# Latent attention on TensorE: the product of weights and values, from full precision to three products of high and low parts

## The chip, the cores and the metric

The kernel runs on one core of one Trainium2 chip. The metric is the device time of one execution in microseconds (us). A core has a matrix engine (TensorE, PE in the profile, with its weight loads shown apart as PEld), a vector engine (VectorE, DVE), an activation engine (ScalarE, ACT), GpSimd (POOL) and the queue that issues DMAs (SyncE, SP). The engines run their own instruction streams side by side and wait for one another by semaphores.

## The reference, cut to what matters

The reference is two transformer blocks over 512 latent and 256 context tokens, then a routed layer of experts. The change is in the second layer of the first block, a latent attention of 8 heads over all 768 tokens as keys:

```python
def mla_core(q, k, v):
    s = jnp.einsum('bqhd,bkhd->bhqk', q, k).astype(F32) * ((C_NOPE + C_ROPE) ** -0.5)
    p = jax.nn.softmax(s, axis=-1)
    return jnp.einsum('bhqk,bkhd->bqhd', p.astype(v.dtype), v)

def keys_values(ckv, k_rope, length):
    kv = (rms_norm(ckv, kv_norm_w) @ wkv_b).reshape(bsz, length, C_HEADS, C_NOPE + C_V)
    ...
```

Queries and keys have 128 + 64 features to a head, values 128. The second `einsum` of `mla_core` (weights times values) is what the change computes in another way.

## The kernel before, in words

Everything is float32 in memory. A product of two float32 matrices is made in one of two ways. In the first, the operands are declared F32 and TensorE does the multiplication in full precision; the trace then has two MATMUL records (and two LDWEIGHTS records) for each such instruction of the program. In the second, each operand is split into a high part (ScalarE copies the value into a tile of the type F32R, which rounds it) and a low part (VectorE subtracts the high part from the value), and TensorE makes three F32R products: high by high, high by low, low by high. Each of these has one record. The large projections (`three`, lines 2106 to 2108) and the scores of this attention (`odd_scores`, lines 2309 and 2316) are made in the second way. The product of weights and values (line 2292) is made in the first.

The latent attention handles the 8 heads in two groups `g` of four. For each group PE makes queries (`q`, six column blocks), their rotations (`rope`), keys (`kv`, four blocks) and values (`v`, six token tiles of 512 columns). ScalarE makes high parts of queries and keys, VectorE their low parts (`low`, line 1592); the values are only copied by ScalarE into `v_o` (line 1047).

Then come 16 units, one for each of four query tiles and four heads, handled in pairs by `attend_pairs`. For a pair PE runs: six transposes of the exponentials `po` for each unit (jobs "T", line 2160), the scores of the next pair (jobs "S", `odd_scores`), and six products of transposed weights with values for each unit (jobs "O", line 2292). Around it, VectorE takes the maximum of each row of scores (`maximum`, line 1530), ScalarE takes the exponential (`exps`, line 1022) into `po`, and copies each finished transpose from PSUM into `pto` (line 1055); VectorE scales the output by the reciprocal of the sum (`scaled_out`, lines 1536 and 1538). PSUM has four slots of two banks. `begin` of a job waits until the job before it in its slot was evacuated. The units' "S" jobs use slots 0 and 1; "T" and then "O" of a unit share slot 2 or 3, so an "O" waits for the evacuation of its own unit's "T".

VectorE and ScalarE are strictly in order. VectorE's list for a pair is: two maxima of the next pair, two `scaled_out`, in group 1 for every second pair a multiplication of a row tile by the gate (line 1625), and then side work: for the first two pairs of a group the low parts of the weights streamed for later stages (`low_part`, line 1246), for the next six partial sums for a modulation vector (`add_part`, lines 1291 and 1293). The last pair of a group has no scores of a next pair between its "T" and its "O".

The stages after this attention (projection out, second block, experts) start only from its output rows `oo_rows`.

Of the kernel before, what the change touches and what calls it, by code (L numbers as in the profile page):

```python
# [16 lines left out]
P = 128  # L17
# [275 lines left out]
def build(nc, src, out):  # L293
# [8 lines left out]
    with ExitStack() as stack:  # L302
# [58 lines left out]
        v_o = at("v_o", g_base, 0, [P, NT, 512])  # L361
# [7 lines left out]
        po, pto = [], []  # L369
        for g in range(2):  # L370
            used = plan.splits[plan.through["q", g] - 1]["k"] % SPLIT
            po.append(at(f"po{g}", split_base, 8 * KB * used, [P, 3, TOK]))
            pto.append(at(f"pto{g}", split_base, 8 * KB * (SPLIT + used), [P, 2, TOK]))
        y_in = at("y_in", split_base, 8 * KB * (SPLIT + used) + 8 * KB, [P, 2, D])

        qa = at("qa", g_base, 0, [P, LT, 512])
        kk = at("kk", g_base, 8 * KB, [P, NT, 512])
# [477 lines left out]
        def _(act):  # L855
# [160 lines left out]
            def exps(stage, u, pbuf, nb):  # L1016

                if u % S_RUN[stage] >= 3:
                    filled(act, "T", stage, u - 3)
                act.wait_ge(nb, u + 1)  # L1020
                st = soft[:, u % 4, :]
                own.free(nc.scalar.activation(pbuf[:, u % 3, :], slot(("S", stage, u))[:, 0:TOK], ACT.Exp, bias=st[:, 1:2],
                                         accum_out=st[:, 2:3]), ev("S", stage, u))

            for g in range(2):
                for f in Q_ORDER:
                    v = filled(act, "q", g, f)
                    if f < 4:
                        own.free(nc.scalar.activation(q_h[:, f, :], v[:, 0:SEQ], ACT.Copy, scale=O_SCALE), s_q_hi)
                        if g == 0 and f == 1:  # L1030
                            split_high(("kv", 0))
                        continue
                    if g == 0:
                        act.wait_ge(s_y[f % 2], 16 * 4)
                    own.free(nc.scalar.activation(tmp[:, f - 4, 0:SEQ], v[:, 0:SEQ], ACT.Copy, scale=O_SCALE), ev("q", g, f))
                if g == 0:
                    act.wait_ge(s_kr, 1)
                    own.free(nc.scalar.activation(kr_h[:], kr_t[:], ACT.Copy), s_kr_hi)
                for f in range(4):
                    v = filled(act, "kv", g, f)  # L1040
                    own.free(nc.scalar.activation(k_h[:, f, :], v[:, 0:TOK], ACT.Copy), s_q_hi)
                for j in range(2):
                    act.wait_ge(s_qr, 2 * g + j + 1)
                    own.free(nc.scalar.activation(qr_h[:, j, :], tmp[:, j, 0:SEQ], ACT.Copy), s_qr_hi)
                for m in range(NT):
                    v = filled(act, "v", g, m)
                    own.free(nc.scalar.activation(v_o[:, m, :], v[:, 0:512], ACT.Copy), ev("v", g, m))
# [187 lines left out]
        def _(dve):  # L1235
# [353 lines left out]
            def low(job, high, part, n, width, factor):  # L1589
# [2 lines left out]
                own.free(nc.vector.scalar_tensor_tensor(part, v[:, 0:width], factor, high.bitcast(F32), ALU.mult, ALU.subtract),  # L1592
                         ev(*job))

            for g in range(2):
                for f in range(4):
                    low(("q", g, f), q_h[:, f, :], q_l[:, f, :], 8 * g + f + 1, SEQ, O_SCALE)
# [5 lines left out]
                for j in range(2):  # L1603
                    rotate(("rope", "qr", 2 * g + j), tmp[:, j, 0:SEQ], q_spin[:, j, :], s_qr)
                for f in range(4):
                    low(("kv", g, f), k_h[:, f, :], k_l[:, f, :], 8 * g + f + 5, TOK, 1.0)
                for j in range(2):
                    dve.wait_ge(s_qr_hi, 2 * g + j + 1)
                    own.free(nc.vector.tensor_tensor(qr_l[:, j, :], tmp[:, j, 0:SEQ], qr_h[:, j, :].bitcast(F32),
                                                     ALU.subtract), s_qr_lo)  # L1610
                if g:
                    ada(2, 2)
                maximum("odd", 16 * g, s_nbo)
                maximum("odd", 16 * g + 1, s_nbo)
                for i in range(8):
                    u = 16 * g + 2 * i
                    if i < 7:
                        maximum("odd", u + 2, s_nbo)
                        maximum("odd", u + 3, s_nbo)
# [435 lines left out]
        def _(pe):  # L2055
# [221 lines left out]

            banks = ((0, 512), (512, TOK))

            def attend_pairs(stage, units, score, pbuf, pts, v_of, n, between=None):  # L2280

                score(units[0])
                for u in units[::2]:
                    for w in (u, u + 1):
                        evacuated(pe, "S", stage, w)
                        turn(("T", stage, w), [pbuf[:, w % 3, P * a:P * a + P] for a in range(NT)], [P * a for a in range(NT)])
# [8 lines left out]
                    if between and u == between[0]:  # L2295
                        between[1]()

            passes = ((0, 0), (0, 1), (1, 0))

# [19 lines left out]
            for g in range(2):  # L2319
# [35 lines left out]
                attend_pairs("odd", range(16 * g, 16 * g + 16), odd_scores, po[g], [pto[g][:, 0, :], pto[g][:, 1, :]],  # L2355
                             lambda u, a: v_o[:, a, P * (u % 4):P * (u % 4) + P], P)
# [415 lines left out]
```

## Time and profile before

| | |
|---|---|
| Time, median of 3 runs | 1785.51 us (1783.41 to 1790.7) |
| Time of the profiled execution | 1785.85 us |
| Span of the profiled execution | 1784.1 us |
| PE busy | 1573.7 us, 88% |
| DVE busy | 918.4 us, 51% |
| ACT busy | 532.5 us, 30% |
| Groups of the latent attention, units only | from 654 to 719 us and from 744 to 809 us of the span |
| PE's share of the chain that ended last | 56% |

The profile shows one execution. The span begins with the first instruction and is 1.75 us shorter than the time of the same execution. In the busy row of PE a matmul counts from its issue to its modelled end, so pipelined matmuls overlap; what one costs in a row of many is read from the distance between starts. "Idle before" names what an engine waited for.

### The profile page before, as it was taken

To read this page: it belongs to the slowest core of one execution; us is meant where nothing else is said; L and a number is where in the kernel's file an instruction comes from. 1 tells how busy PE (TensorE), PEld (TensorE's weight loads), DVE (VectorE), ACT (ScalarE), POOL (GpSimd) and SP (SyncE) were. 2 spreads that over 40 slices of the span, in tenths; PEclk is the share of its full clock that TensorE was granted. 3 is DMA by queue.
4 is the path that set the end of the run, shared out by engine and by line. 5 is a ranking of instruction groups with operands and counts; after the bars stand their busy time and mean duration, and the time that the engine had idled before them with its cause. 6 is when DMAs were issued, how large, how long until landed. Compare 5 with 4: busy or idle time off the path is not lost.

```text
span 1784.1 us, 22804 instructions
## 1 busy us (share of the span) xinstructions
PE 1573.7 (88%) x8464; PEld 1119.4 (63%) x8464; DVE 918.4 (51%) x1595; ACT 532.5 (30%) x844; POOL 180.7 (10%) x263
## 2 busy tenths in 40 slices
PE   6699999799799989999899888796999898989880
PEld 6588888578688868788788677675443333333330
DVE  3876537566548645577587887754121111111125
ACT  3312222367233354544522475121111101101011
POOL 2000010023110100001202300110000000000002
PEclk9899999869899999999899999895999999999995
DMA  9132355100332311223434012235999999999984
GB/s 374 70 120 95 124 190 188 53 13 13 124 118 74 134 65 48 95 83 142 161 142 168 22 48 96 105 127 218 401 423 423 422 422 423 423 422 423 422 355 147
DMA packets 55794, 353.06 MB, mean 198 GB/s; under 512 B 7408, under 2 KB 7664, under 8 KB 18720
## 3 DMA queue, kind: packets, MB, share of 16 engines
q1 hardware_dynamic: 43056, 306.88, 42.9%
q0 software_dynamic: 12656, 45.07, 6.8%
q8 instruction: 53, 0.87, 0.2%
q14 instruction: 29, 0.24, 0.0%
HBM read 332.26 MB, written 23.59 MB: 199 GB/s over the span
## 4 chain that ended last, share of the span: by engine, by line
PE 56%; DMA 17%; DVE 16%; ACT 4%; issue 3%; SPq 3%; POOL 0%; DVEq 0%; POOLq 0%; ACTq 0%
PE ps L2106 10%; DMA early<-in_experts 10%; PE ps L2108 10%; PE ps L2107 10%; PE ps L2595 6%; PE ps L2160 3%; DMA raw<-in_experts 3%; PE ps L2616 3%; PE ps L2292 3%; SPq L657 2%; PE ps L2576 2%; PE ps L2316 2%; PE ps L2085 2%; DVE stat L1530 1%; ACT p L938 1%
## 5 line engine op out<-in xcount | busy, mean ns | idle before, releaser
L2106 PE MATMUL ps<-whi,xth 128*128 128x512 f32 (+1 forms) x768 | 304.0, 396 | 11.8 <-DVE xtl L1642 5.4
L2107 PE MATMUL ps<-wlo,xth 128*128 128x512 f32 (+1 forms) x768 | 300.1, 391 | 0.0
L2108 PE MATMUL ps<-whi,xtl 128*128 128x512 f32 (+1 forms) x768 | 300.0, 391 | 0.0
L2006 DVE TENSOR_TENSOR hid<-hid,ps 128x256 f32<-128x256 f32 x33 | 13.9, 421 | 370.5 <-ACT hid L1197 370.5
L2106 PEld LDWEIGHTS ps<-whi,xth 128*128 128x128 f32 x768 | 147.6, 192 | 42.2 <-DVE xtl L1642 5.7
L2108 PEld LDWEIGHTS ps<-whi,xtl 128*128 128x128 f32 x768 | 147.0, 191 | 30.3
L2107 PEld LDWEIGHTS ps<-wlo,xth 128*128 128x128 f32 x768 | 147.4, 192 | 28.6
L2595 PE MATMUL ps<-early,xe_t 128*64 128x512 f32 x624 | 142.3, 596 | 13.9 <-DMA early<-in_experts 12.8
L1246 DVE TENSOR_TENSOR wlo<-raw,whi 128x2048 fp32r<-128x2048 f32 (+3 forms) x52 | 103.1, 1983 | 69.3 <-ACT whi L867 63.1
L867 ACT ACTIVATE whi<-raw 128x2048 fp32r<-128x2048 f32 (+2 forms) x46 | 85.5, 1858 | 120.9 <-DMA raw<-in_even 33.4
L2595 PE MATMUL ps<-raw,xe_t 128*64 128x512 f32 x432 | 101.1, 600 | 19.1 <-DMA raw<-in_experts 16.2
L2595 PEld LDWEIGHTS ps<-early,xe_t 128*64 128x64 f32 x624 | 43.0, 137 | 109.5 <-issue 74.1
L1293 DVE SCALAR_TENSOR_TENSOR raw<-raw,cvec 128x512 f32<-128x512 f32 x140 | 105.2, 752 | 4.9
L2616 PE MATMUL ps<-early,hid_t 128*64 128x512 f32 x408 | 94.8, 601 | 1.7 <-DVE hid_t L2010 0.5
L1530 DVE TENSOR_REDUCE stat<-ps 128x1 f32<-128x768 f32 x64 | 61.2, 956 | 55.5 <-PE ps L2309 50.3
L1197 ACT ACTIVATE hid<-ps 128x256 f32<-128x256 f32 x33 | 12.7, 384 | 254.0 <-PE ps L2595 254.0
L2595 PEld LDWEIGHTS ps<-raw,xe_t 128*64 128x64 f32 x432 | 28.2, 136 | 89.2 <-issue 45.1
L835 POOL DMA_DIRECT2D pair_dram<-tmp x66 | 34.5, 523 | 470.6 <-ACT tmp L1202 467.5
L2576 PE MATMUL ps<-h2h,hot 128*128 128x512 f32 x144 | 60.8, 422 | 6.1 <-DVE hot L1994 6.1
L684 POOL TENSOR_SCALAR stat<-stat 128x1 f32<-128x1 f32 (+3 forms) x36 | 12.0, 333 | 520.4 <-ACT xtl_f L966 154.1
L1202 ACT ACTIVATE tmp<-ps 128x512 f32<-128x512 f32 x33 | 19.7, 597 | 136.8 <-PE ps L2616 136.8
L2616 PEld LDWEIGHTS ps<-early,hid_t 128*64 128x64 f32 x408 | 26.4, 136 | 51.0 <-issue 45.5
(445 smaller groups left out, 2809.8 us busy)
## 6 DMA issues: line engine op xcount, KB each, us to landing
early<-in_experts SPq DMA_DIRECT2D x129, 1024.0 KB, 26.1
raw<-in_experts SPq DMA_DIRECT2D x54, 1024.0 KB, 26.0
raw<-in_ada SPq DMA_DIRECT2D x40, 1024.0 KB, 6.5
ring<-in_experts SPq DMA_DIRECT2D x15, 1024.0 KB, 27.6
raw<-in_even SPq DMA_DIRECT2D x14, 1024.0 KB, 5.6
raw<-in_second SPq DMA_DIRECT2D x10, 1024.0 KB, 5.0
pair_dram<-tmp POOLq DMA_DIRECT2D x66, 128.0 KB, 5.8
early<-in_ada SPq DMA_DIRECT2D x8, 1024.0 KB, 18.2
```

Source lines behind the costliest of these rows:

```text
L867: own(nc.scalar.activation(whi[:, k % SPLIT, 0:w], raw[:, number[splits[k]["name"]] % RAW, 0:w], ACT.Copy), s_hi)
L1246: own(nc.vector.tensor_tensor(wlo[:, k % SPLIT, at_], raw[:, g % RAW, at_], whi[:, k % SPLIT, at_].bitcast(F32), ALU.subtract), s_lo if pa ...
L1293: ins = nc.vector.scalar_tensor_tensor(dst, w[kt // 4][:, kt % 4, :], cv, dst, ALU.mult, ALU.add)
L1530: own(nc.vector.tensor_reduce(st[:, 1:2], v[:, 0:TOK], AX, ALU.max, negate=True), nb)
L2106: nc.tensor.matmul(v, a[0], b[0], start=first, stop=False)
L2107: nc.tensor.matmul(v, a[0], b[1], start=False, stop=False)
L2108: return nc.tensor.matmul(v, a[1], b[0], start=False, stop=last)
L2160: mm = nc.tensor.transpose(v[:, to:to + P], rows_, ident[:])
L2292: mm = nc.tensor.matmul(v[:, TOK:TOK + n], pts[w % 2][:, P * a:P * a + P], v_of(w, a), start=a == 0, stop=a == NT - 1)
L2576: mm = nc.tensor.matmul(ps[:, h, :], hot[:, m, :], part[:, m, 512 * h:512 * h + 512], start=m == 0 and part is h2h, stop=m == LT - 1 and p ...
L2595: mm = nc.tensor.matmul(ps[SLOT * t:SLOT * t + SLOT, 4 + s, :], xe_t[:, 2 * i + k, SLOT * s:SLOT * s + SLOT], w[:, D * k + 512 * t:D * k + ...
L2616: mm = nc.tensor.matmul(ps[SLOT * t:SLOT * t + SLOT, 7, :], hid_t[:, s, P * c + SLOT * k:P * c + SLOT * k + SLOT], w[:, D * k + 512 * t:D ...
```

## The change

The function `attend_pairs` becomes `odd_pairs(g)`. The weights by key and the values now have high and low parts. ScalarE's copies are the same in number and size but write F32R tiles (`v_h`, `pto_h`) and no longer free the PSUM slot. VectorE then subtracts the high part from the PSUM value into the low part (`v_l`, `pto_l`) and frees the slot. PE makes three F32R products for each block of 128 keys in place of one F32 product. The exponentials use `tmp` for two of their three buffers, and low parts of values and weights lie in split buffers whose weights are no longer needed; the transfers and their order are unchanged.

```diff
@@ scalar
                 for m in range(NT):
                     v = filled(act, "v", g, m)
-                    own.free(nc.scalar.activation(v_o[:, m, :], v[:, 0:512], ACT.Copy), ev("v", g, m))
+                    own.free(nc.scalar.activation(v_h[:, m, :], v[:, 0:512], ACT.Copy), s_q_hi)
@@
-                        own.free(nc.scalar.activation(pto[g][:, n % 2, :], v[:, 0:TOK], ACT.Copy), ev("T", "odd", n))
+                        own.free(nc.scalar.activation(pto_h[g][:, n % 2, :], v[:, 0:TOK], ACT.Copy), s_q_hi)
@@ vector
+                for m in range(NT):
+                    low(("v", g, m), v_h[:, m, :], value_low(g, m), HIGHS * g + m + 9, 512, 1.0)
                 if g:
                     ada(2, 2)
                 maximum("odd", 16 * g, s_nbo)
                 maximum("odd", 16 * g + 1, s_nbo)
                 for i in range(8):
                     u = 16 * g + 2 * i
+                    for n in (u, u + 1):
+                        if i:
+                            filled(dve, "O", "odd", n - 2)
+                        low(("T", "odd", n), pto_h[g][:, n % 2, :], pto_l[g][:, n % 2, :], HIGHS * g + 15 + n % 16, TOK, 1.0)
                     if i < 7:
                         maximum("odd", u + 2, s_nbo)
                         maximum("odd", u + 3, s_nbo)
@@ tensor
                     for w in (u, u + 1):
-                        v = begin("O", stage, w)
+                        v = begin("O", "odd", w)
+                        keys = [x[g][:, w % 2, :] for x in (pto_h, pto_l)]
+                        at_ = slice(P * (w % 4), P * (w % 4) + P)
                         for a in range(NT):
-                            mm = nc.tensor.matmul(v[:, TOK:TOK + n], pts[w % 2][:, P * a:P * a + P], v_of(w, a),
-                                                  start=a == 0, stop=a == NT - 1)
-                        end(mm, "O", stage, w)
+                            values = (v_h[:, a, at_], value_low(g, a)[:, at_])
+                            for n, (i, j) in enumerate(passes):
+                                mm = nc.tensor.matmul(v[:, TOK:TOK + P], keys[i][:, P * a:P * a + P], values[j],
+                                                      start=a + n == 0, stop=a == NT - 1 and n == 2)
+                        end(mm, "O", "odd", w)
```

`low` itself is as before; the two constants `8 * g` in its older calls become `HIGHS * g`, since more high parts are counted by the same semaphore:

```python
            def low(job, high, part, n, width, factor):
                v = filled(dve, *job)
                dve.wait_ge(s_q_hi, n)
                own.free(nc.vector.scalar_tensor_tensor(part, v[:, 0:width], factor, high.bitcast(F32), ALU.mult, ALU.subtract),
                         ev(*job))
```

## Rows read from the trace of the kernel before

**Rows 1.** Page, the chain that ended last by engine.

```profile
PE 56%; DMA 17%; DVE 16%; ACT 4%; issue 3%; SPq 3%; POOL 0%; DVEq 0%; POOLq 0%; ACTq 0%
```

**Rows 2.** Chain of one pair of units: start us, us, what.

```profile
695.58 2.88 PE ps L2292 x24
698.45 1.45 PE ps L2160 x12
699.91 1.39 PE ps L2316 x6
...
703.64 2.88 PE ps L2292 x24
```

**Rows 3.** Timeline of the same pair: start us, us, engine, line, operation, count.

```profile
695.51 2.94 PE L2292 MATMUL ps<-v_o,pto 128*128 128x128 f32 x24
695.68 1.95 DVE L1530 TENSOR_REDUCE stat<-ps 128x1 f32<-128x768 f32 x2 [2.47 <-PE ps L2309]
...
697.73 0.90 ACT L1022 ACTIVATE po<-ps,stat 128x768 f32<-128x768 f32 x1
...
698.33 1.34 PEld L2160 LDWEIGHTS ps<-ident,po 128*128 128x128 f32 x12
...
698.95 2.33 DVE L1293 SCALAR_TENSOR_TENSOR acc<-raw,cvec,acc 128x512 f32<-128x512 f32 x3
...
699.64 0.19 PEld L2316 LDWEIGHTS ps<-k_h,q_h 128*128 128x128 f32 x1
```

**Rows 4.** Groups by line and form, 655 to 820 us: count, busy us, mean ns.

```profile
L2292 PE MATMUL ps<-v_o,pto 128*128 128x128 f32 x384 | 47.1, 280 | 0.4 <-ACT pto L1055 0.4
```

**Rows 5.** Timeline of weight loads: F32R loads for 256 columns, F32 loads for one.

```profile
694.05 0.19 PEld L2316 LDWEIGHTS ps<-k_h,q_h 128*128 128x128 f32 x1 [0.36 <-issue]
694.16 0.19 PEld L2316 LDWEIGHTS ps<-k_l,q_h 128*128 128x128 f32 x1
...
694.51 0.28 PE L2316 MATMUL ps<-k_h,q_h 128*128 128x256 f32 x1
...
694.63 0.28 PE L2316 MATMUL ps<-k_l,q_h 128*128 128x256 f32 x1
...
739.65 0.30 PEld L2085 LDWEIGHTS ps<-half,acc 128*128 128x128 f32 x2
...
740.32 0.30 PEld L2085 LDWEIGHTS ps<-half,raw 128*128 128x128 f32 x2
```

**Rows 6.** Lines 1592 (low parts), all its instructions: ns minimum, median, maximum.

```profile
L1592 DVE SCALAR_TENSOR_TENSOR q_l<-ps,q_h x8: 690/692/693, 631.1 to 728.1; 128x512 fp32r<-128x512 f32 x8
L1592 DVE SCALAR_TENSOR_TENSOR k_l<-ps,k_h x8: 945/946/957, 643.2 to 735.7; 128x768 fp32r<-128x768 f32 x8
```

**Rows 7.** Timeline between the values and the first scores of both groups.

```profile
646.68 1.28 DVE L1609 TENSOR_TENSOR qr_l<-tmp,qr_h 128x512 fp32r<-128x512 f32 x2
...
650.35 0.47 PE L2316 MATMUL ps<-k_h,q_h 128*128 128x512 f32 x1 [1.20 <-ACT v_o L1047]
...
736.54 1.28 DVE L1609 TENSOR_TENSOR qr_l<-tmp,qr_h 128x512 fp32r<-128x512 f32 x2
...
740.57 0.48 PE L2316 MATMUL ps<-k_h,q_h 128*128 128x512 f32 x1
```

**Rows 8.** Timeline of the last pair of group 0.

```profile
714.46 1.34 PEld L2160 LDWEIGHTS ps<-ident,po 128*128 128x128 f32 x12
...
715.08 2.33 DVE L1293 SCALAR_TENSOR_TENSOR raw<-raw,cvec 128x512 f32<-128x512 f32 x3
...
716.24 2.75 PEld L2292 LDWEIGHTS ps<-v_o,pto 128*128 128x128 f32 x24 [0.44 <-ACT pto L1055]
```

**Rows 9.** Stretches: length, busy PE, PEld, DVE, ACT, POOL, granted clock, DMA, GB/s.

```profile
656.00:660.00 4.00, 3.62 (x16) 3.11 (x17) 0.29 (x1) 2.94 (x6) 0.00 (x0) 0.60 0.02 4
660.00:700.00 40.00, 40.00 (x300) 33.40 (x299) 22.20 (x39) 19.05 (x32) 0.00 (x0) 1.00 0.16 53
```

**Rows 10.** Chain: the first transposes of group 0, in the first of these stretches.

```profile
656.38 2.53 PE ps L2160 x12
```

More of the change, by code:

```diff
@@ L360, in build @@
         kr_h = at("kr_h", g_base, 45 * KB, [P, TOK], F32R)
-        v_o = at("v_o", g_base, 0, [P, NT, 512])
+        v_h = at("v_h", g_base, 0, [P, NT, 512], F32R)
         k_h = at("k_h", xt_base, 0, [P, 4, TOK], F32R)
@@ L368, in build, with value_low @@
         q_spin = at("q_spin", xt_base, 44 * KB, [P, 2, SEQ])
-        po, pto = [], []
+        po, v_l, pto_h, pto_l = [], [], [], []
         for g in range(2):
             used = plan.splits[plan.through["q", g] - 1]["k"] % SPLIT
-            po.append(at(f"po{g}", split_base, 8 * KB * used, [P, 3, TOK]))
-            pto.append(at(f"pto{g}", split_base, 8 * KB * (SPLIT + used), [P, 2, TOK]))
-        y_in = at("y_in", split_base, 8 * KB * (SPLIT + used) + 8 * KB, [P, 2, D])
+            behind = (used + 1) % SPLIT
+            v_l.append([at(f"v_l{g}", split_base, 8 * KB * used, [P, 4, 512], F32R),
+                        at(f"v_m{g}", split_base, 8 * KB * (SPLIT + used), [P, 2, 512], F32R)])
+            po.append([tmp[:, 0, :], tmp[:, 1, :], at(f"po{g}", split_base, 8 * KB * (SPLIT + used) + 4 * KB, [P, TOK])[:]])
+            pto_h.append(at(f"pto_h{g}", split_base, 8 * KB * behind, [P, 2, TOK], F32R))
+        pto_l = [at("pto_l0", split_base, 8 * KB * (SPLIT + plan.splits[plan.through["q", 0]]["k"] % SPLIT), [P, 2, TOK], F32R),
+                 at("pto_l1", g_base, 20 * KB, [P, 2, TOK], F32R)]
+        y_in = at("y_in", split_base, 8 * KB * (SPLIT + behind), [P, 2, D])
+        def value_low(g, m):
+            return v_l[g][m // 4][:, m % 4, :]
         qa = at("qa", g_base, 0, [P, LT, 512])
@@ L1021, in exps @@
                 st = soft[:, u % 4, :]
-                own.free(nc.scalar.activation(pbuf[:, u % 3, :], slot(("S", stage, u))[:, 0:TOK], ACT.Exp, bias=st[:, 1:2],
+                p = pbuf[u % 3] if stage == "odd" else pbuf[:, u % 3, :]
+                own.free(nc.scalar.activation(p, slot(("S", stage, u))[:, 0:TOK], ACT.Exp, bias=st[:, 1:2],
                                          accum_out=st[:, 2:3]), ev("S", stage, u))
@@ L1593, in low @@
                          ev(*job))
+            HIGHS = 4 + 4 + NT + 16
             for g in range(2):
                 for f in range(4):
-                    low(("q", g, f), q_h[:, f, :], q_l[:, f, :], 8 * g + f + 1, SEQ, O_SCALE)
+                    low(("q", g, f), q_h[:, f, :], q_l[:, f, :], HIGHS * g + f + 1, SEQ, O_SCALE)
                     if g == 0 and f == 1:
@@ L1605, in _ @@
                 for f in range(4):
-                    low(("kv", g, f), k_h[:, f, :], k_l[:, f, :], 8 * g + f + 5, TOK, 1.0)
+                    low(("kv", g, f), k_h[:, f, :], k_l[:, f, :], HIGHS * g + f + 5, TOK, 1.0)
                 for j in range(2):
@@ L2278, in _, with odd_pairs @@
             banks = ((0, 512), (512, TOK))
-            def attend_pairs(stage, units, score, pbuf, pts, v_of, n, between=None):
+            def odd_pairs(g):
+                score = odd_scores
+                units = range(16 * g, 16 * g + 16)
                 score(units[0])
@@ L2284, in attend_pairs @@
                     for w in (u, u + 1):
-                        evacuated(pe, "S", stage, w)
-                        turn(("T", stage, w), [pbuf[:, w % 3, P * a:P * a + P] for a in range(NT)], [P * a for a in range(NT)])
+                        evacuated(pe, "S", "odd", w)
+                        turn(("T", "odd", w), [po[g][w % 3][:, P * a:P * a + P] for a in range(NT)], [P * a for a in range(NT)])
                     if u + 2 in units:
@@ L2289, in attend_pairs @@
                     for w in (u, u + 1):
-                        v = begin("O", stage, w)
+                        v = begin("O", "odd", w)
+                        keys = [x[g][:, w % 2, :] for x in (pto_h, pto_l)]
+                        at_ = slice(P * (w % 4), P * (w % 4) + P)
                         for a in range(NT):
-                            mm = nc.tensor.matmul(v[:, TOK:TOK + n], pts[w % 2][:, P * a:P * a + P], v_of(w, a),
-                                                  start=a == 0, stop=a == NT - 1)
-                        end(mm, "O", stage, w)
-                    if between and u == between[0]:
-                        between[1]()
+                            values = (v_h[:, a, at_], value_low(g, a)[:, at_])
[3 more added lines that the diff above has]
+                        end(mm, "O", "odd", w)
             passes = ((0, 0), (0, 1), (1, 0))
@@ L2354, in _ @@
                 pe.wait_ge(s_qr_lo, 2 * g + 2)
-                attend_pairs("odd", range(16 * g, 16 * g + 16), odd_scores, po[g], [pto[g][:, 0, :], pto[g][:, 1, :]],
-                             lambda u, a: v_o[:, a, P * (u % 4):P * (u % 4) + P], P)
+                odd_pairs(g)
             def gate(layer, first, n=0):
```

## The prediction

> **What bounds the kernel now.** I read the page's chain first: PE carries 56% of what ended last, far ahead of DMA and DVE [rows 1]. Then I looked at the chain inside the latent attention, the only stage the change touches. Rows 2 show one pair of units, and every piece of it is PE: the outputs (line 2292, 24 records), the transposes (line 2160, 12), the scores of the next pair (lines 2316 and 2309, of which the first piece stands there), and the outputs again 8.06 us later. The other pairs, apart from the first and last of each group, repeat this to a hundredth. So in this stage PE is the bound, without a gap, and time goes up or down with what its instructions cost in a row. The timeline of the same pair [rows 3] shows the same from the side of the others: DVE sat idle 2.47 us before the maxima, and ACT's copies of the transposes run under PE's scores. What the reader should take along: the price of the change is set by PE's distance from start to start, and DVE's new work is free only where those idle stretches lie.
>
> **Part 1, the products.** Removed: 192 F32 instructions, which are 384 records of line 2292 [rows 4]. Added: three F32R products for each, 576 records. How far apart are they? The duration in the rows (280 ns) is latency and does not add up. From the first output load at 695.51 to the first transpose load at 698.33 pass 2.82 us for 24 records [rows 3], 117.5 ns for each.
>
> For a F32R product of 128 columns there is no row, so I bound it. Two F32R products of 256 columns start 0.12 us apart (694.51, 694.63), and the first two loads after a break, which have no earlier product to wait for, 0.11 us (694.05, 694.16) [rows 5]. At the other end stand products that stream a single column: their loads go from 739.65 to 740.32 in six steps, 112 ns each [rows 5]. And 12 transposes, each with a fresh load of 128x128, run from 698.33 to 699.64, 109 ns each [rows 3]. So one column, a transpose of 128 and a product of 256 columns all come out between 109 and 118 ns. What they share is a fresh 128x128 load of four-byte weights. I take it that the load sets the distance and that fewer columns than 256 bring nothing. The F32 record at 117.5 ns fits the same picture. I take 112 ns, the row where the load is seen most purely; the ends are 109 and 117.5.
>
> A pair of units then needs 36 x 0.112 = 4.03 us where it needed 2.82, so 1.21 us more; 16 pairs make **+19.4 us** (17.7 at 109 ns, 22.6 at 117.5).
>
> The Trainium skill, page "TensorE: Matmul & The Clock Gate", section "Back-to-back issue gap", gives another figure for a stream of loads and matmuls: about 81 ns for each at 128 columns. By it a pair would need 36 x 0.081 = 2.92 us and this term would be +1.6 us. The rows here speak against it for four-byte weights: none is nearer than 109 ns.
>
> **Part 2, low parts of the weights by key.** 32 instructions of VectorE, 128x768 out of PSUM, like `k_l`: 0.946 us each [rows 6]. An "O" now waits for its unit's low part, since that frees the slot. In an inner pair, let 0 be the start of the transposes (698.33). DVE ends its sums at 701.28, that is 2.95 [rows 3]; ACT's copies are done by then. The two low parts end at 3.9 and 4.9. The outputs start at 5.25 (703.57, as 695.51 + 8.06) [rows 2, 3]. So the first low part has 1.3 us to spare, and the second is needed only when its own outputs start, 2 us later still. What hides them is the scores of the next pair (3.9 us of PE). In group 1 the row multiplication (1.2 us by its size) comes on top of the sums for some pairs; then the first low part ends about 5.1, still in time, and the maxima start up to 0.9 us late. That has cover too: the second exponential ends 3.12 us after the scores do (695.51 to 698.63) [rows 3], and the longer outputs give 4.03 us. DVE's total for the fullest pair, about 8.4 us (two low parts 1.9, two maxima 1.95, scaling 1.0, multiplication 1.2, sums 2.33), is under the new period of 9.3. The inner pairs: 0. If that cover were gone, DVE would set the period; at 8.4 it does not.
>
> The last pair of each group has no scores between transposes and outputs. There the outputs started at 716.24, 1.78 after the transposes [rows 8]. Now DVE first finishes the three sums (to 717.41) and then the low part (to 718.4), so the outputs start at about 718.5: +2.2 us, and the same in group 1. What is queued behind that wait is everything PE still has to do. Together **+4.4 us** (from 3.0, if the sums start earlier against the transposes, to 5.5).
>
> **Part 3, low parts of the values.** 12 instructions of 128x512, 0.692 us each [rows 6]. They stand in DVE's list behind the low parts of keys and rotated queries, which end at 647.96 in group 0 and 737.82 in group 1 [rows 7]. Six at 0.70 end at about 652.2 and 742.0; the scores wait for all six, as before for ACT's copies. PE started them at 650.35 and 740.57 [rows 7]. With 0.1 to 0.5 us from release to start that is +2.2 and +1.8, **+4.0 us** (2.5 to 6). The upper end has PE's clock in it: after a pause of 2.1 us before the first transposes the granted clock was 0.60 of full over 656 to 660 us, between its two levels of 1.2 and 2.4 GHz, and 1.00 afterwards [rows 9]. A second pause of 2 us stands before the scores now, which may cost another 2 us at the half clock; I leave this out of the sum and in the range.
>
> **The rest.** ACT's copies keep number and size and only write another type, so 0. Other buffers, same transfers, same queues: 0, with nothing new to hide. The stages after the attention read its output rows and move back as a whole; the transfers they wait for are issued behind PE's jobs, so no wait there takes up the delay.
>
> Sum: 19.4 + 4.4 + 4.0 = 27.8 us. Against the profiled execution, 1785.85 (its span is 1784.1), that is 1813.6. The median of the runs is 0.34 lower, so **1813.3 us**; the bounds of the terms give 1785.5 + 23.2 = 1809 and 1785.5 + 34.1 = 1820, to 1824 with the clock.
>
> **The rivals.**
>
> A. *The loads hide and the columns set the distance.* From 512 to 256 columns the distance falls from 0.23 us (1.39 us for six in rows 2) to 0.12, so 128 columns would take about 0.062 us and the outputs of a pair 2.24 us, 0.58 less. But then another chain decides: the second exponential ends 3.12 us after the scores, and its transposes began only 0.36 us later than that (698.33 + 0.65). So a pair gains at most 0.36 us. 14 pairs give 5.0, the last two 1.2, against 8.4 us of new waits: +2.2, **1788 us**, no change that a measurement shows. It decides if the distance is under about 85 ns. For it speaks that fewer columns are streamed; against it the one-column row and the transposes. Here belongs the skill's 81 ns, which would give 1.6 + 8.4 = +10, 1796 us. Not slower needs this; clearly faster needs, besides, that the waits of parts 2 and 3 do not come. Chance 0.14.
>
> B. *A F32R product of few columns is not one pass.* If each product took two records as an F32 one does, a pair would need 72 x 0.1175 = 8.46 us, +5.64, 16 pairs +90, and with the waits **1884 us**. For it: the kernel has no F32R product under 256 columns, so no row excludes it. Against: all F32R rows have one record each. Chance 0.08.
>
> C. *The clock falls in the outputs*, as PE streams fewer columns in the same time. At the half level a record would take about 211 ns (the twelve transposes in the stretch at 0.60 took 2.53 us against 1.45 [rows 2, 10]), 36 of them 7.6 us: +57 us, **about 1870 us**. Against it: the transposes stream as little and stay at 1.00 in 660 to 700 us [rows 9]. Chance 0.04.
>
> **How the numbers follow.** The forecast (parts 1 to 3) has 0.74, with its own range 1808 to 1824. With A it makes 0.88, so the range is 1789 to 1824, without B and C. A measurement tells about 0.5% (8.9 us) from no change: under 1776.6 is faster, over 1794.4 slower. Slower: 0.74 + 0.08 + 0.04 and the part of A near 81 ns, 0.03, 0.89. Same: 0.10. Faster: 0.01.
>
> **What would show it.** In the profile after: 576 records of the output line, whose 36 for a pair span 3.9 to 4.3 us (2.3 would be A, 8 B or C, which the granted clock tells apart). Period of an inner pair 9.2 to 9.4 us against 8.06, still all PE in the chain. The last pair of each group shows PE waiting some 2 us for DVE's low part, and so do the first scores. DVE never on the chain in inner pairs; if it is there, part 2 is wrong. Nothing after the attention changes length.

## The result

The changed kernel takes 1828.92 us, median of 4 runs (1827.61 to 1830.15), against 1787.01 us in the runs of the kernel before beside it. The ratio is 1.0239, with a 95% interval of 1.0224 to 1.0255: slower by 2.4%, or about 42 us. The forecast was slower by 28 us, 1813.3 us, with an upper bound of 1824. The direction is right, the size is too small by a third, and the time lies outside the range.

The profiled execution took 1829.32 us (span 1827.6). The page's chain has 57% PE, as against 56% [rows 1]. First the chain inside an inner pair and the last pair of group 0 (start us, us, what), which answers to rows 2 and 8:

```profile
692.67 0.55 PE ps L2330 x6
693.22 4.17 PE ps L2315 x36
697.38 1.45 PE ps L2177 x12
698.84 1.37 PE ps L2337 x6
700.21 0.90 PE ps L2330 x6
701.11 0.91 PE ps L2337 x6
702.02 0.55 PE ps L2330 x6
702.57 4.17 PE ps L2315 x36
...
727.52 0.76 DVE raw L1303
728.30 0.97 DVE pto_l L1602
729.32 6.92 PE ps L2315 x36
736.24 0.53 PE ps L2123
736.77 0.43 PE ps L2124
```

Line 2315 is now the output product. Inner pairs (all but the first and the last of a group) look as foreseen: all PE, period 9.35 us. The last pair does not. Its chain goes through VectorE, as foreseen, but then the same 36 records take 6.92 us in place of 4.17, and the projection products behind them stand 0.43 us apart in place of 0.23.

The single products (timeline of PE: start, us, ...), two in an inner stretch, the first after the pause, and two from the slow part:

```profile
721.37 0.28 PE L2315 MATMUL ps<-v_l,pto_h 128*128 128x128 f32 x1
721.48 0.27 PE L2315 MATMUL ps<-v_h,pto_l 128*128 128x128 f32 x1
...
729.32 0.33 PE L2315 MATMUL ps<-v_h,pto_h 128*128 128x128 f32 x1 [2.42 <-DVE pto_l L1602]
...
732.20 0.41 PE L2315 MATMUL ps<-v_h,pto_h 128*128 128x128 f32 x1
732.41 0.41 PE L2315 MATMUL ps<-v_l,pto_h 128*128 128x128 f32 x1
```

A product is 0.11 us from the next at first, and 0.21 in the slow part. The stretches (length, busy PE, PEld, DVE, ACT, POOL, granted clock, DMA share, GB/s) show why:

```profile
721.00:726.00 5.00, 5.00 (x48) 4.75 (x44) 3.00 (x7) 1.98 (x4) 0.00 (x0) 1.00 0.00 2
726.00:729.30 3.30, 0.90 (x8) 0.64 (x6) 3.19 (x5) 1.59 (x2) 0.00 (x0) 1.00 0.00 0
729.30:736.00 6.70, 6.68 (x36) 6.69 (x37) 1.41 (x4) 0.00 (x0) 0.00 (x0) 0.59 0.01 2
736.00:742.00 6.00, 6.00 (x19) 4.78 (x19) 3.38 (x6) 1.20 (x2) 0.00 (x0) 0.61 0.00 0
```

The granted clock is 1.00 (2.4 GHz) up to the pause and is at the lower level (1.2 GHz) for most of the outputs and for the first 4.7 us of the projection behind them.

For an account I cut the attention at events that both traces have: the first low part of the keys in each group, the first scores, the first outputs, the last pair's outputs, the next stage, and the transfer of the output weights issued behind the attention. All numbers are differences of start times in us; "alone" is the first experiment below, which has the new products but none of VectorE's new work.

| stretch | before | after | alone |
|---|---|---|---|
| group 0: keys' low parts to first scores | 7.14 | 9.33 | 7.14 |
| first scores to first outputs | 12.90 | 14.51 | 13.07 |
| first outputs to the last pair's | 52.99 | 64.23 | 62.00 |
| last pair's outputs | 2.70 | 6.72 | 4.07 |
| queries, rotations of group 1 | 14.14 | 16.30 | 14.10 |
| group 1: keys' low parts to first scores | 7.49 | 9.07 | 7.49 |
| first scores to first outputs | 11.65 | 13.02 | 11.65 |
| first outputs to the last pair's | 53.00 | 64.25 | 61.96 |
| last pair's outputs | 2.78 | 6.86 | 4.08 |
| gate, transposes, sums | 7.90 | 9.49 | 7.89 |
| sum | 172.7 | 213.8 | 193.5 |

The attention took 41.1 us longer, of the 43.5 us between the two spans. The granted clock over the whole of it was 0.99 before, 0.93 after and 0.99 for the products alone; by the trace's record of the clock PE stood at the lower level for 3.4, 30.7 and 3.4 us of it. The stages ahead of it and behind it issue the same instructions. Those ahead took 643.2 us before and 641.3 after, those behind 968.2 and 972.6, together 1611.4 and 1613.8.

### The profile page after: what moved, and what is told of

Same layout as the page of the kernel before. It is cut to its first block, busy times and chain, and to the rows that moved or that the text cites. A ratio compares the mean times of both kernels' runs of the same rounds, so it can differ in the third digit from the quotient of the medians.

```text
span 1827.6 us, 23274 instructions
## 1 busy us (share of the span) xinstructions
PE 1610.6 (88%) x8656; PEld 1153.1 (63%) x8656; DVE 954.0 (52%) x1639; ACT 533.4 (29%) x844; POOL 181.0 (10%) x263
## 4 chain that ended last, share of the span: by engine, by line
PE 57%; DMA 16%; DVE 15%; ACT 4%; issue 3%; SPq 3%; POOL 0%; DVEq 0%; POOLq 0%; ACTq 0%
PE ps L2123 10%; DMA early<-in_experts 10%; PE ps L2125 10%; PE ps L2124 10%; PE ps L2615 6%; PE ps L2315 4%; PE ps L2177 3%; DMA raw<-in_experts 3%; PE ps L2636 3%; SPq L666 2%; PE ps L2596 2%; PE ps L2337 2%; PE ps L2102 2%; DVE stat L1540 1%; PE ps L2330 1%
## 5 line engine op out<-in xcount | busy, mean ns | idle before, releaser
L2023 DVE TENSOR_TENSOR hid<-hid,ps 128x256 f32<-128x256 f32 x33 | 13.9, 421 | 371.8 <-ACT hid L1207 371.8
L1207 ACT ACTIVATE hid<-ps 128x256 f32<-128x256 f32 x33 | 12.7, 384 | 255.3 <-PE ps L2615 255.3
L2315 PE MATMUL ps<-v_h,pto_h 128*128 128x128 f32 x192 | 56.1, 292 | 4.8 <-DVE pto_l L1602 4.8
```

The source lines that it names most:

```text
L2315: mm = nc.tensor.matmul(v[:, TOK:TOK + P], keys[i][:, P * a:P * a + P], values[j], start=a + n == 0, stop=a == NT - 1 and n == 2)
```

## The experiments

Ten kernels ran. For each, "attention" is the sum of its stretches as in the table above. Whole times are medians of 4 runs, except where one is named, and everything on the attention is read from one profiled execution of each kernel; the kernel before had 1785.1 to 1786.5 us beside them. The code shows the lines that matter, with `...` where others are left out.

**1. The products alone.** ScalarE frees the slots again; the low parts are left out, and PE reads high parts in their place.

```diff
-own.free(nc.scalar.activation(pto_h[g][:, n % 2, :], v[:, 0:TOK], ACT.Copy), s_q_hi)
+own.free(nc.scalar.activation(pto_h[g][:, n % 2, :], v[:, 0:TOK], ACT.Copy), ev("T", "odd", n))
...
-keys = [x[g][:, w % 2, :] for x in (pto_h, pto_l)]
+keys = [x[g][:, w % 2, :] for x in (pto_h, pto_h)]
...
-values = (v_h[:, a, at_], value_low(g, a)[:, at_])
+values = (v_h[:, a, at_], v_h[:, a, at_])
```

> Left out: both sets of low parts. ScalarE frees the PSUM slots as before the change, and the second and third product of each block read the high parts again, so PE's instructions and shapes are those of the changed kernel with none of VectorE's new work. Theory (the products cost their load, and the granted clock falls after the pauses that VectorE's low parts make): outputs of an inner pair 4.1 to 4.2 us, the pause before the last pair's outputs 0.2 us, the last pair's outputs also 4.1 to 4.2 us at a granted clock of 1.00; in all 16 x 1.3 = 21 us over the kernel before, about 1808 us. Rival (the clock falls because narrow products stream less, pause or not): last pair's outputs about 6.9 us, and the next stage starts at the low clock, about 1817 us.

The attention took 193.5 us, 20.8 over the kernel before. The chain (start us, us, what) at an inner pair's outputs and at the last pair's:

```profile
722.41 4.17 PE ps L2311 x36
728.15 4.24 PE ps L2311 x36
```

And the stretch around the last pair's outputs (length, busy PE, PEld, DVE, ACT, POOL, granted clock, DMA share, GB/s):

```profile
728.00:734.00 6.00, 5.88 (x45) 5.55 (x45) 3.48 (x8) 1.02 (x3) 0.00 (x0) 1.00 0.01 3
```

So the products cost 20.8 us, and by themselves they do not lower the clock: it stays at 1.00, and the last outputs take what the others take. The rival of this run falls. The whole took 1831.64 us, which no longer measures the products: without the low parts other numbers leave the attention, the router of the layer behind it hands out one more block of experts, and PE has 1088 records of expert inputs (632 and 456) where the kernel before has 1056 (624 and 432). The same holds for experiments 2 and 3 (1842.36 and 1835.25 us), so of these three only the attention is read, and their expectations for the whole time are neither met nor refuted.

**2 and 3. One set of low parts at a time.** In the second experiment the values' low parts are left out, in the third those of the weights by key, each by the lines above that concern it.

> Left out: the low parts of the values (12 instructions of VectorE); ScalarE frees those slots, and the second product reads the high part of the values. Theory: the scores of both groups start some 2.2 and 1.4 us earlier against the keys' low parts, and what the half clock cost after that pause (1.6 and 1.5 us up to the first outputs) goes in part; 3.6 to 6.7 us under the changed kernel, 1822 to 1825 us. Rival (those low parts were hidden): 1829 us.

> Left out: the low parts of the weights by key (32 instructions of VectorE); ScalarE frees those slots, and the third product reads the high part again. Theory: the pause before the last outputs of each group goes from 2.4 to 0.2 us, and with it the half clock in these outputs and behind them (2.9 + 3.1 us in the outputs, 2.0 and 1.3 behind): 4.4 + 9.3 = 13.7 us under the changed kernel, about 1815 us. Rival (the clock falls from narrow products): only the 4.4 us go, about 1824.5 us, and the last outputs still take 6.9 us.

| kernel | attention | last outputs, group 0 and 1 | scores to first outputs |
|---|---|---|---|
| after | 213.8 | 6.72, 6.86 | 14.51, 13.02 |
| no low values | 207.4 | 6.68, 7.30 | 13.03, 11.66 |
| no low weights | 199.7 | 4.07, 4.07 | 14.42, 13.07 |
| neither | 193.5 | 4.07, 4.08 | 13.07, 11.65 |

The low parts of the values cost 6.4 us (6.3 when taken from the third kernel), those of the weights by key 14.1 us (13.9). The two add up with the 20.8 us of the products to the 41.1. Each is more than its waits: 3.8 us of waits for the values (2.19 and 1.58 in the first table), 4.5 us for the weights by key (2.23 and 2.29). The rest, 12 us, is PE at the lower clock: these four kernels spent 30.7, 23.9, 10.2 and 3.4 us of the attention at that level, in the order of the table.

**4. A shorter pause.** VectorE makes the last pair's low parts ahead of the three sums.

```diff
                     else:
+                        if i == 6:
+                            weights_low(g, u + 2)
                         for n in range(16 * (i - 2) // 6, 16 * (i - 1) // 6):
                             add_part(2, 2 + g, n)
```

> The full computation. Only VectorE's order is changed: the low parts of the last pair's weights come ahead of the three partial sums. Theory: they end 0.95 us after ScalarE's first copy, so the outputs start about 1.3 us earlier and the pause is 1.1 us in place of 2.4; if a pause of this length keeps the clock at 1.00, the whole is 2 x 1.3 + 9.3 = 12 us under the changed kernel, 1817 us. Rival (narrow products lower the clock): only 2.6 us, 1826 us. A third outcome, the clock falling after 1.1 us as well, would look like the rival and be told from it by the first run of this set.

1823.73 us, ratio to the kernel before 1.0208 (1.0189 to 1.0228); attention 206.3 us. The pause shrank from 2.4 to 1.2 us in each group, and yet the clock fell: the last outputs took 6.09 and 6.40 us. It is the third outcome that the expectation named. With a pause of 0.2 us or less (the kernel before, experiments 1 and 3) the clock held, with 1.2 us it did not. Of the 7.5 us saved, 2.4 are the pause and 2.0 lie between scores and first outputs, which this edit does not touch (experiment 9 comes back to that stretch).

**5. The same pause in the kernel before.** VectorE copies the last pair's transposes in place of ScalarE, behind its sums; the outputs stay F32 products.

```diff
+                        if u % 16 < 14:
+                            own.free(nc.scalar.activation(pto[g][:, n % 2, :], v[:, 0:TOK], ACT.Copy), ev("T", "odd", n))
...
+                    if i == 7:
+                        for n in (u, u + 1):
+                            v = filled(dve, "T", "odd", n)
+                            filled(dve, "O", "odd", n - 2)
+                            own.free(nc.vector.tensor_scalar(pto[g][:, n % 2, :], v[:, 0:TOK], 1.0, None, ALU.mult), ev("T", "odd", n))
```

> The kernel before, full computation, with one edit: for the last pair of each group VectorE copies the transposes in place of ScalarE, in its order behind the three sums. The outputs stay F32 products. Theory (a pause of PE of over 2 us lowers the clock whatever stands behind it): the pause before the last outputs grows from 0.2 to about 2.2 us, the granted clock falls during these outputs, which take 4.5 to 5.5 us against 2.7, and the next stage starts at the low level; 2 x 2.1 + 4 to 9 us over the kernel before, 1795 to 1800 us. Rival (the narrow F32R products are needed for the fall): the outputs stay at 2.7 us at a clock of 1.00, and only 4.2 us are lost, 1790.6 us.

1795.27 us, ratio 1.0056 (1.0039 to 1.0073); attention 178.2 us, 5.5 over the kernel before, 4.5 of them pause. The stretches in group 0:

```profile
712.00:716.00 4.00, 1.58 (x14) 1.28 (x13) 3.70 (x7) 0.33 (x2) 0.00 (x0) 0.94 0.00 0
716.00:719.50 3.50, 3.50 (x19) 3.50 (x20) 1.30 (x4) 0.00 (x0) 0.00 (x0) 0.58 0.00 0
719.50:728.00 8.50, 8.50 (x43) 7.15 (x42) 4.09 (x8) 2.99 (x5) 0.00 (x0) 1.00 0.00 0
```

The clock fell here too, in group 0, but was back at 1.00 before the projection began; the last outputs took 4.12 us (2.70 before) and in group 1 2.78, as before. Neither side of the expectation is right: a pause alone can lower the clock, but behind it the F32 outputs lost 1.4 us in all where the three narrow products and what follows lost 4.8 in group 0 and 4.4 in group 1. Two pauses in one execution do not show that the type of the products makes this difference; experiment 7 has F32R products, the same pause, and one group of two in which the clock held.

**6. Products of 64 columns.** Only half of each head's value features is computed, written twice.

```diff
-at_ = slice(P * (w % 4), P * (w % 4) + P)
+at_ = slice(P * (w % 4), P * (w % 4) + 64)
...
-mm = nc.tensor.matmul(v[:, TOK:TOK + P], keys[i][:, P * a:P * a + P], values[j],
+mm = nc.tensor.matmul(v[:, TOK:TOK + 64], keys[i][:, P * a:P * a + P], values[j],
```

> The changed kernel with products of 64 columns in place of 128: only the first 64 value features of a head are computed, and VectorE writes them twice. What comes after the attention gets other numbers, so only the attention is to be read. Theory (the load sets the distance): products stay 0.111 us apart, 36 of them 4.1 to 4.2 us, period of an inner pair 9.35 us. Rival (columns set it): 0.06 us apart or less, the period falls by 1.5 us or more. If 128 columns were bound by columns in several passes, half of them would halve the distance.

There is one run, of 1851.07 us, of which only the attention is read. Two neighbours in the timeline of PE (start us, us, what):

```profile
698.08 0.28 PE L2315 MATMUL ps<-v_l,pto_h 128*128 128x64 f32 x1
698.19 0.28 PE L2315 MATMUL ps<-v_h,pto_l 128*128 128x64 f32 x1
```

They start 0.11 us apart, as with 128 columns. So the columns do not set the distance, and rival A of the prediction falls; the load, which has kept its size, fits. And yet the attention took 238.2 us, 24.4 more than the changed kernel with twice the columns. The stretch that holds most of group 0's pairs (columns as above):

```profile
665.00:740.00 75.00, 74.00 (x468) 64.96 (x467) 43.46 (x69) 27.07 (x44) 0.00 (x0) 0.80 0.09 29
```

The changed kernel has 0.94 over the same stretch, its slow last pair included. The chain says what that costs (two pairs):

```profile
697.68 4.38 PE ps L2315 x36
702.06 2.63 PE ps L2177 x12
...
708.56 4.98 PE ps L2315 x36
713.54 2.63 PE ps L2177 x12
```

The transposes behind the outputs, which the edit does not touch, take 2.63 us; they take 1.45 at the full clock and took 2.53 in the slow stretch of the kernel before [rows 2, 10]. So with 64 columns PE fell to the lower level inside the pairs, where it has no pause at all. In the changed kernel the inner pairs stay at 1.00. Rival C, that narrow products lower the clock by themselves, is thus seen at 64 columns and not at 128.

**7. Fewer loads.** The high and low part of a value tile lie side by side, so one product of 256 columns takes both against the high weights, and one of 128 takes the high values against the low weights: 24 loads for a pair, as many as the kernel before has records. VectorE adds the two halves as it scales.

```diff
-values = (v_h[:, a, at_], value_low(g, a)[:, at_])
-for n, (i, j) in enumerate(passes):
-    mm = nc.tensor.matmul(v[:, TOK:TOK + P], keys[i][:, P * a:P * a + P], values[j],
-                          start=a + n == 0, stop=a == NT - 1 and n == 2)
+values = value_parts(g, a)[:, :, at_]
+nc.tensor.matmul(v[:, TOK:TOK + 2 * P].rearrange("p (b n) -> p b n", b=2),
+                 keys[0][:, P * a:P * a + P], values, start=a == 0, stop=False)
+mm = nc.tensor.matmul(v[:, TOK:TOK + P], keys[1][:, P * a:P * a + P], values[:, 0, :],
+                      start=False, stop=a == NT - 1)
...
-scaled_out("odd", n, oo_rows[:, m, P * h:P * h + P], P, TOK)
+own(nc.vector.tensor_scalar(dst, v[:, TOK:TOK + P], st[:, 3:4], None, ALU.mult))
+own(nc.vector.scalar_tensor_tensor(dst, v[:, TOK + P:TOK + 2 * P], st[:, 3:4], dst, ALU.mult, ALU.add),
+    ev("O", "odd", n))
```

> The full computation. High and low parts of a value tile lie side by side, and one product of 256 columns makes high x high and high x low at once, in two regions of PSUM; low x high is the second product; VectorE adds the two regions while scaling (one more instruction of 128x128 for a unit, about 0.38 us). So 24 loads for a pair in place of 36. Theory (loads are what is paid for, up to about 256 columns): 12 x (0.118 + 0.111) = 2.75 us for the outputs of a pair, the period back to 8.0 to 8.1 us in pairs where VectorE is not full, up to 9.2 in the two fullest of group 1; the pauses and their clock stay. About 20 us under the changed kernel, 1805 to 1809 us. Rival (columns count): the streamed columns are the same 384 for a key block, so the outputs stay at 4.2 us and the time at 1829 us or above.

1815.03 us, ratio 1.0161 (1.0143 to 1.0179); attention 198.0 us, 15.8 less than the changed kernel. The timeline of PE:

```profile
695.02 0.34 PE L2324 MATMUL ps<-v_b,pto_h 128*128 128x256 f32 x1
695.20 0.23 PE L2326 MATMUL ps<-v_b,pto_l 128*128 128x128 f32 x1
695.26 0.33 PE L2324 MATMUL ps<-v_b,pto_h 128*128 128x256 f32 x1
...
697.45 0.74 PE L2187 MATMUL ps<-ident,po 128*128 128x128 f32 x5 [0.18 <-DVE oo_rows L1648]
```

One key block with its two products takes 0.23 us (695.02 to 695.26, and 2.83 us for the 12 blocks of the last pair of group 0). That is two loads' worth, though the 256 columns stream as well, against 0.33 for three loads. So a pair saves 1.3 us of PE, its outputs take what the F32 ones took, and three loads in place of two are what the 20.8 us are made of. But the period of a pair is 8.65 us, not 8.1, and 9.2 to 9.3 us for three pairs of group 1. The last row shows PE waiting for a scaling instruction of VectorE, and the chain (start us, us, what) shows why:

```profile
702.45 0.56 PE ps L2341 x5
703.01 0.02 issue
703.03 0.97 DVE stat L1544
704.00 0.02 issue
704.02 0.97 DVE stat L1544
...
705.21 0.36 DVE oo_rows L1647
705.58 0.03 issue
705.60 0.36 DVE oo_rows L1648
705.96 0.14 issue
706.10 0.85 PE ps L2187 x6
```

The transposes need the slot that holds the previous outputs, and DVE reads it only behind two maxima (0.97 us each). With PE 1.3 us faster this order of DVE's is on the path: its price is 0.6 us for each pair and 1.2 for those three, some 9 us in all. That is enough for the 6 us by which the time lies over the upper end that the expectation gave.

The last outputs took 2.83 us in group 0, where the clock held, and 5.18 in group 1, where it fell, though the pause ahead of them is 2.41 us in both. In the three long pairs of group 1 PE waits up to 0.8 us ahead of the transposes, and the clock does not fall. The row of one such wait, and the stretch that holds this group's pairs up to the last (columns as above):

```profile
789.71 0.84 PE L2187 MATMUL ps<-ident,tmp 128*128 128x128 f32 x6 [0.76 <-DVE oo_rows L1648]
...
764.30:829.00 64.70, 58.46 (x420) 47.40 (x418) 56.23 (x91) 29.48 (x46) 1.57 (x3) 1.00 0.17 58
```

**8. PE busy in the pause.** Nine products that nothing reads stand between the last pair's transposes and its outputs.

```diff
 if u + 2 in units:
     score(u + 2)
+if u + 2 not in units:
+    for n in range(9):
+        nc.tensor.matmul(slot_at(n % 2)[:, 0:512], k_h[:, n % 4, 0:P], k_h[:, n % 4, P:P + 512], start=True, stop=True)
 for w in (u, u + 1):
     v = begin("O", "odd", w)
```

> The full computation, with nine products of 512 columns (0.23 us each, 2.05 us) whose result nobody reads, issued by PE in the pause before the last outputs of each group. Nothing starts earlier by it. Theory (PE's idle time lowers the clock): with the rest of the pause 0.4 us, the clock stays at 1.00, the last outputs take 4.1 us and not 6.7 to 6.9, the stages behind them start at full clock; 2.65 + 2.2 + 2.8 + 1.6 = 9.2 us under the changed kernel, 1819.7 us. Rival (narrow products lower the clock): no gain, 1829 us.

The timeline of PE, and the stretch behind it:

```profile
725.57 2.33 PE L2310 MATMUL ps<-k_h 128*128 128x512 f32 x9
728.23 0.33 PE L2318 MATMUL ps<-v_h,pto_h 128*128 128x128 f32 x1 [0.33 <-DVE pto_l L1602]
```

(columns of the next row as in the stretches above)

```profile
728.00:734.00 6.00, 5.77 (x44) 5.49 (x45) 2.98 (x8) 0.07 (x1) 0.00 (x0) 1.00 0.01 3
```

The outputs wait for the same low part, but the clock stays at 1.00, and they take 4.07 and 4.08 us in place of 6.72 and 6.86. The stretches behind them take 14.07 and 7.54 in place of 16.30 and 9.49. Together 9.6 us, and the attention took 204.1, 9.7 less. The fill leaves the start of the last outputs where it was (64.27 and 64.31 us behind the first ones, as against 64.23 and 64.25) and changes only what PE does while it waits. So those 9.6 us are the clock's, and here PE's idle time brought it down. The whole time moved less: 1824.17 us, ratio 1.0224 (1.0207 to 1.0242), 4.7 under the changed kernel.

**9. PE busy in both pauses.** Thirteen unread products of 256 columns behind the values as well, ahead of the scores.

```diff
+for n in range(13):
+    nc.tensor.matmul(v[:, 768:1024], ckvh[:, 0:P], ckvh[:, P:P + 256], start=True, stop=True)
```

> The full computation, as the run with nine unread products in the pause before the last outputs, and with 13 more of 256 columns (1.5 us) in the pause behind the values, before the first scores of each group. Theory (PE's pauses, not VectorE's work itself, bring the half clock): 33.7 us of the attention's 41.1 us stay at most; the stretch from the first scores to the first outputs takes 12.9 us in group 0 and 11.65 us in group 1, as in the kernel before, against 14.5 and 13.0 us; 9.7 + up to 3 us under the changed kernel, about 1817 to 1820 us. Rival (these stretches are slow for another reason): they stay as they are, 1820 us or more.

1822.67 us, ratio 1.0197 (1.0176 to 1.0219); attention 204.0 us, as in experiment 8. The stretches around the scores, in group 0 and 1:

| kernel | keys' low parts to scores | scores to first outputs |
|---|---|---|
| after | 9.33, 9.07 | 14.51, 13.02 |
| experiment 8 | 9.34, 9.05 | 12.89, 14.45 |
| experiment 9 | 9.31, 10.14 | 13.01, 13.20 |

The second fill brought nothing in all. In group 1 it even delayed the scores by 1.1 us, since the products stand ahead of PE's next job there. The right column also shows a limit of this study: without any edit near them, this stretch took 14.5 and 12.9 us in group 0 of two kernels, and 13.0 and 14.5 in group 1. The granted clock goes with it. The stretches, group 0 and 1 of the kernel before and of experiment 8 (columns as above):

```profile
650.35:663.25 12.90, 10.83 (x60) 7.96 (x61) 1.92 (x2) 4.33 (x7) 0.00 (x0) 0.87 0.01 1
740.57:752.22 11.65, 9.39 (x62) 6.68 (x61) 2.08 (x3) 3.58 (x6) 1.14 (x3) 1.00 0.91 360
...
651.06:663.95 12.89, 10.82 (x60) 8.07 (x60) 3.83 (x4) 3.60 (x6) 0.00 (x0) 0.87 0.01 1
755.42:769.87 14.45, 12.30 (x61) 9.06 (x61) 3.83 (x4) 3.60 (x6) 0.69 (x2) 0.76 0.73 289
```

The stretch takes some 11.6 us at 1.00, 12.7 to 13.3 at about 0.87 and 14.3 to 14.5 at 0.76, in all twelve kernels. Without the wait for the low values it was 0.87 and 1.00 in the groups of all four kernels; with that wait, and without a fill there, the two groups together always lost more. Why it is this group or that, I did not find.

**10. All of it.** The wide products, the last pair's low parts first, and fills of 3 and 13 products.

> The full computation: high and low values side by side with one product of 256 columns and one of 128 (24 loads for a pair), the last pair's low parts ahead of the sums, and unread products in both pauses (three of 512 and 13 of 256 columns). Theory: from the 198.0 us of the attention stretch in the wide kernel go 2.6 us of pause, 2.4 + 0.7 us of half clock at the end and up to 4 us of it before the first outputs: 188 to 191 us against 172.7 before and 213.8 after the change, so 1801 to 1805 us. Faster than the kernel before would need loads to be saved against its 24 for a pair, and there are 24 here as well; so no gain over it is expected.

1809.83 us, ratio 1.0133 (1.011 to 1.0156), where 1801 to 1805 were expected; attention 191.1 us, at the upper end of the 188 to 191 expected, 22.7 less than the changed kernel and still 18.4 more than the kernel before. The last outputs took 2.83 us in both groups. Most of what is left over the kernel before is VectorE: 11.8 us between the first outputs and the last pair's, with pairs of 8.65 us, up to 9.26 in group 1, that its order sets, and 4.8 us ahead of the scores, of which 1.1 are the fill's delay. No version here is faster than the kernel before.

## Why the prediction was too small

**What bounds the kernel, and the rivals.** The reading of [rows 1 to 3] held: the inner pairs are all PE, their period is 9.35 us (9.2 to 9.4 foreseen), and DVE is never on their chain. Part 2's cover for the inner pairs was right. Rival A needed 62 ns for a product; measured are 112 (the median distance of two starts at the full clock), at 128 and at 64 columns. Rival B falls: each product has one record. The Trainium skill, page "TensorE: Matmul & The Clock Gate", section "Back-to-back issue gap", gives some 81 ns, and no run here shows that for four-byte weights. The Trainium skill, same page, section "LDWEIGHTS (loading the stationary operand)", has a load of 128 columns take its columns over 1.2 GHz, 107 ns. The 112 ns measured at the full clock are near that; the 0.21 us measured at the lower level are not.

**Part 1, the products.** +19.4 foreseen, +20.8 measured in experiment 1. The distance was taken as 112 ns and is 112. But 2.82 us for the 24 removed records is not 24 distances of 117.5 ns: they too stand 112 ns apart, except for 0.21 us where the second unit begins, and the rest lies ahead of the transposes. The new 36 were counted at the bare distance, 4.03 us, with nothing for either. Like for like, a pair went from a period of 8.06 to 9.35 us, 1.29 more and not 1.21, and 16 times 0.08 us makes 1.3 of the 1.4 us.

**Waits.** Last pairs +4.4 foreseen, 4.5 measured (2.23 and 2.29). Low values +4.0 foreseen, 3.8 measured (2.19 and 1.58). The two sets of low parts and the products add up, as the sum assumed.

**The step that failed** is the price of the new pause. Part 2 priced the last pair's wait by its length alone, and what is queued behind it at the durations that the rows had at full clock. Part 3 did know the clock, but set it outside the sum, at up to 2 us for a group (the 1824 of the range), and only at the other pause, the one ahead of the scores. Measured are 12 us in all (213.8 less 193.5, less the 8.3 of waits): 5.4 in the last pairs' outputs, 3.8 in the stretches behind them, and some 2.8 between scores and first outputs. With these 12 the sum would be 27.8 + 12 = 39.8 us; the measured difference is 41.1 within the attention, and the products' 1.4 us are the rest. Experiment 8 shows 9.6 of them (its own figures, 0.4 more than the 5.4 and 3.8 against experiment 1) to hang on PE's idle time ahead of the last outputs. Rival C had the clock, but with another cause and in another place: at 128 columns it does not fall throughout the outputs, which would be +57, but behind the pause. What spoke for pricing it was in the rows: [rows 9] had the clock at 0.60 after a pause of 2.1 us, and [rows 10] what a record costs then. The same trace also shows that it is not certain: ahead of the first transposes of group 1 stands the same pause, 2.13 us, and the clock there is 1.00 (experiment 9's rows).

"Nothing after the attention changes length" is not borne out to the microsecond. The stages behind it took 968.2 us before and 972.6 after; the stages ahead of it, where there is nothing new, took 643.2 and 641.3. Single executions differ that much by themselves: the stages ahead, the same in all twelve kernels, took from 639.5 to 646.2 us, the three shortest with 61 us at the lower level, the three longest with 78 to 82. So a few microseconds outside the attention can't be laid to an edit. This bears on the experiments, too, where the gain in the attention (one execution) and in the whole time (medians) part: 9.7 and 4.7 us in experiment 8, 7.5 and 5.2 in 4, 15.8 and 13.9 in 7, 22.7 and 19.1 in 10, and a loss of 5.5 and 10.2 in 5. All five lie on one side, so there may be more to it than chance; what, is open.

## What to carry to other kernels

A product of 128 or fewer columns with a fresh load of four-byte weights cost 112 ns here whatever its columns; count loads, not columns, and three narrow products in place of two records cost half as much again. When an edit makes PE wait, price the wait and then, as a risk beside it, the work behind it at the lower clock; here the second was more than the first for the last pairs (9.2 us against 4.5). Products that nothing reads, put into such a pause, kept the clock up, but the kernel gains by them only what the clock took.

## What the hardware showed

- With the three narrow products behind it, a pause of 2.4 us brought the granted clock down for some 10 us in both groups of two kernels (the changed one and experiment 2), and one of 1.2 us (experiment 4) brought it down in both groups. Pauses of at most 0.33 us ahead of the last outputs did so in none of twelve cases (the kernel before, experiments 1, 3, 8, 9 and 10), nor did pauses of up to 0.8 us ahead of transposes (experiment 7).
- The same pause of 2.4 us ahead of F32 outputs (experiment 5) and ahead of products of 256 and 128 columns (experiment 7) lowered the clock in one group and cost nothing in the other. Nor did the pauses of 2.1 us ahead of the first transposes, which every kernel has, always lower it. Whether the products behind decide, or the moment at which the pause falls, was not tried.
- With 64 columns the clock fell in the inner pairs with no pause, to 0.80 on the mean of one execution, so that halving the columns cost 24.4 us.
- At the lower level the distance of the narrow products is 0.21 us in place of 0.11: what sets it, by experiments 6 and 7 the load, halves its speed with the clock, too.
- A layout with the values as the loaded side and several query tiles streamed would, by count, need fewer loads; it was not tried.
